# Reordering steps around each head's first scores, and the casts of the last head's output tiles

## The reference

```python
def diff_attend(q, k, v, lam):          # 8 heads, two softmax maps of 64 features each
    def block(qi):                      # 128 queries at a time
        s = jnp.einsum('bqhmd,bkhmd->bhmqk', qi, k).astype(jnp.float32) * scale
        p = jax.nn.softmax(s, axis=-1)
        a = (p[:, :, 0] - lam * p[:, :, 1]).astype(v.dtype)
        return jnp.einsum('bhqk,bkhd->bqhd', a, v)
...
ks_, qs: rope_2d for the latent tokens; k_all, v_all = cache (128 keys) + 512 latent keys
of = of * lax.rsqrt(jnp.mean(jnp.square(of), axis=-1, keepdims=True) + EPS) * subln_w
of = of * (1.0 - lam_init)
return of.astype(o.dtype).reshape(B, L, DA_V) @ w_o
```

## Time and profile before

| | us |
|---|---|
| median of the runs | 1765.52 |
| lowest, highest | 1765.09, 1766.39 |
| the profiled execution, its own time | 1772.52 |
| its span, first to last instruction | 1770.7 |
| TensorE busy in it | 1704.0 (96%) |
| VectorE, ScalarE, GpSimd busy | 1082.0, 703.2, 639.8 |
| attention heads, from the first scores to the last turned tile | about 59.8 to 357.3 |

### The profile page before, as it was taken

The page is one execution under the profiler, slowest core; times in us unless marked ns, Lnnn a source line. Parts: engine busy times, 40 slices in busy tenths (PEclk is TensorE's granted clock), DMA queues, the critical chain, the costliest instruction groups (busy, mean ns, idle before and its releaser), DMA issues.

```text
span 1770.7 us, 30194 instructions
## 1 busy us (share of the span) xinstructions
PE 1704.0 (96%) x11440; PEld 1601.7 (90%) x11440; DVE 1082.0 (61%) x1760; ACT 703.2 (40%) x1142; POOL 639.8 (36%) x317
## 2 busy tenths in 40 slices
PE   6999999899999999999999899999999999999996
PEld 4888888599998999889998899998999999999996
DVE  2677677757766515667367554645878771477824
ACT  4455555536323212232246544554463331133324
POOL 4222112256433433323454222123745333333344
PEclk8999999999999999999999999999999999999998
DMA  9312222521454223443221112211202222122221
GB/s 363 124 54 71 68 63 67 206 83 49 154 203 167 82 73 119 169 188 128 82 69 54 63 54 71 74 48 42 96 25 71 81 80 77 64 79 71 84 82 60
DMA packets 59768, 170.96 MB, mean 97 GB/s; under 512 B 7944, under 2 KB 20488, under 8 KB 59664
## 3 DMA queue, kind: packets, MB, share of 16 engines
q1 hardware_dynamic: 51584, 163.33, 26.6%
q10 hardware_dynamic: 8080, 6.18, 1.1%
HBM read 161.07 MB, written 4.74 MB: 94 GB/s over the span
## 4 chain that ended last, share of the span: by engine, by line
PE 69%; DVE 10%; ACT 6%; DVEq 5%; issue 4%; POOL 4%; ACTq 1%; DMA 1%; SPq 0%; POOLq 0%
PE pj L752 57%; POOL wlo L629 3%; DVEq L2298 2%; PE psO L1004 2%; PE mO L1237 2%; PE pfrow L777 1%; DVE pr L2312 1%; ACT pr L1569 1%; POOL ss L643 1%; PE psS L969 1%; DVE sm L2297 1%; DVEq L2311 1%; PE mS L1193 1%; ACT whi L1375 1%; PE psT L1012 1%
## 5 line engine op out<-in xcount | busy, mean ns | idle before, releaser
L591 POOL TENSOR_TENSOR wlo<-wraw,whi 128x1024 fp32r<-128x1024 f32 (+1 forms) x120 | 310.5, 2588 | 789.5 <-ACT whi L1375 787.4
L752 PE MATMUL pj<-Hh,whi 128*128 128x320 f32 x2240 | 536.7, 319 | 13.8 <-ACT Hh L1550 4.0
L752 PE MATMUL pj<-Hl,whi 128*128 128x320 f32 x2240 | 517.0, 311 | 1.4 <-POOL Hl L614 1.1
L752 PE MATMUL pj<-Hh,wlo 128*128 128x320 f32 x2240 | 518.1, 310 | 0.0
L752 PEld LDWEIGHTS pj<-Hh,whi 128*128 128x128 f32 x2240 | 375.6, 190 | 40.3 <-issue 29.7
L752 PEld LDWEIGHTS pj<-Hl,whi 128*128 128x128 f32 x2240 | 377.6, 189 | 2.4 <-POOL Hl L614 2.0
L752 PEld LDWEIGHTS pj<-Hh,wlo 128*128 128x128 f32 x2240 | 379.2, 189 | 0.3
L1375 ACT CAST whi<-wraw 128x1024 fp32r<-128x1024 f32 (+1 forms) x168 | 187.2, 1114 | 261.5 <-PE pj L752 227.7
L2218 DVE SCALAR_TENSOR_TENSOR fcv<-fus,vec,fcv 128x127 f32<-128x127 f32 (+1 forms) x176 | 222.3, 1304 | 15.1 <-issue 15.1
L752 PE MATMUL pj<-Gh,whi 128*128 128x320 f32 x704 | 168.5, 310 | 0.8 <-POOL wlo L629 0.8
L2080 DVE SCALAR_TENSOR_TENSOR X<-pj,mods,X 128x128 f32<-128x128 f32 (+5 forms) x114 | 43.1, 433 | 205.8 <-PE pj L752 205.6
(11 more groups left out here) (367 smaller groups left out, 2370.5 us busy)
## 6 DMA issues: line engine op xcount, KB each, us to landing
wraw<-in_w_up SPq DMA_DIRECT2D x84, 512.0 KB, 3.5
fwr<-in_w_ada SPq DMA_DIRECT2D x56, 512.0 KB, 5.2
wraw<-in_w_dn SPq DMA_DIRECT2D x32, 704.0 KB, 4.1
wraw<-in_w_qkv SPq DMA_DIRECT2D x24, 512.0 KB, 3.5
wraw<-in_w_mlin SPq DMA_DIRECT2D x24, 512.0 KB, 3.5
awr<-in_w_ada SPq DMA_DIRECT2D x16, 512.0 KB, 10.4
awr<-in_w_ada SPq DMA_DIRECT2D x16, 256.0 KB, 8.0
wraw<-in_w_wo SPq DMA_DIRECT2D x8, 512.0 KB, 3.6
```

Of the source, the lines that this page charges most:

```text
L591: nc.gpsimd.tensor_tensor(wlo[k][:, 0:width], wraw[k][:, 0:width], whi[k][:, 0:width].bitcast(F32), ALU.subtract).then_inc(w_lo, 1)
L752: last = mm(out[:, c, 0:HALF], w, x[:, j, c * HALF:(c + 1) * HALF], start=(j == 0 and n == 0), stop=(j == n_k - 1 and n == 2))
```

## The change

Five edits, all in layer 0's attention:

1. TensorE, `head` and `last_head`: step 7 of the query unit (in the last head: of the last value unit) goes ahead of `scores(h, 0)`.
2. VectorE, `head`: `turned(h, 3)` goes ahead of `q_lo(h + 1)`.
3. ScalarE, `last_head`: `unit_split(U_WO + 1)` goes from behind `o_square` to right behind `exps(h, 0)`.
4. ScalarE, `last_head`: the six `output_hi` casts move forward: tiles 0 and 1 behind `values_hi`, tile 2 behind `o_out(h - 1)`, tile 3 behind `exps(h, 2)`, tiles 4 and 5 behind `exps(h, 3)`.
5. GpSimd: the eight `Hl` subtractions are written out instead of a loop, and those of tiles 3, 4 and 5 wait for `nmax_ready` of score tiles 2, 3 and 4 of the last head as well.

```diff
+            def part_lo_split(n):
+                pool.wait_ge(part_hi, n + 1)
+                nc.gpsimd.tensor_tensor(wlo[0][:, 0:CUT * P], ...).then_inc(part_lo, 1)
...
-            output_lo(O32, 1, 0, KT)
+            for j in range(KT):
+                pool.wait_ge(h_hi, KT + j + 1)
+                if j in (3, 4, 5):
+                    pool.wait_ge(nmax_ready, 5 * (DA_HEADS - 1) + j)
+                nc.gpsimd.tensor_tensor(Hl[:, j, :], O32[:, j, :], Hh[:, j, :].bitcast(F32), ALU.subtract).then_inc(o_ready, 1)
+            part_lo_split(0)
...
+                qkv(q, [7])
                 scores(h, 0)
                 if h == 0:
                     ada_turn(3)
-                qkv(q, [7])
...
             def last_head(h):
+                qkv(3 * DA_HEADS - 1, [7])
                 scores(h, 0)
-                qkv(3 * DA_HEADS - 1, [7])
...
                 exps(h, 0)
+                unit_split(U_WO + 1)
                 values_hi(h)
+                output_hi(O32, onorm, (0, 1))
                 o_out(h - 1, (L0, L0 + LAT), 1)
+                output_hi(O32, onorm, (2,))
                 turned(h, 0)
                 exps(h, 1)
                 o_square(h - 1)
-                unit_split(U_WO + 1)
                 turned(h, 1)
                 exps(h, 2)
                 o_out(h, (C0, C0 + CTX), 0)
-                output_hi(O32, onorm, (0, 1))
+                output_hi(O32, onorm, (3,))
                 turned(h, 2)
                 exps(h, 3)
-                output_hi(O32, onorm, (2, 3))
+                output_hi(O32, onorm, (4, 5))
                 turned(h, 3)
                 exps(h, 4)
                 rms(h - 1)
-                output_hi(O32, onorm, (4, 5))
...
                 nmax(h, 4)
+                turned(h, 3)
                 q_lo(h + 1)
-                turned(h, 3)
                 k_lo(h + 1)
                 values_lo(h)
```

More of the change, by code:

```diff
@@ L607, in split_ffn @@
                 out_split(b + 2 * GH, n, WMAX, 0)
+            def part_lo_split(n):
+                pool.wait_ge(part_hi, n + 1)
+                nc.gpsimd.tensor_tensor(wlo[0][:, 0:CUT * P], wraw[0][:, 0:CUT * P], whi[0][:, 0:CUT * P].bitcast(F32),
+                                        ALU.subtract).then_inc(part_lo, 1)
             def output_lo(src, h_inst, n, early):
@@ L615, in output_lo @@
                 loop(pool, early, body)
-                pool.wait_ge(part_hi, n + 1)
-                nc.gpsimd.tensor_tensor(wlo[0][:, 0:CUT * P], wraw[0][:, 0:CUT * P], whi[0][:, 0:CUT * P].bitcast(F32),
-                                        ALU.subtract).then_inc(part_lo, 1)
+                part_lo_split(n)
                 for j in range(early, KT):
```

## The result

The changed kernel runs in 1761.82 us (median of 11 executions, 1758.1 to 1764.13). The kernel before, on the same chips in the same rounds, has 1771.19 (11 executions, 1765.09 to 1773.84). The ratio is 0.9949, 95% interval 0.9938 to 0.9961: 9.0 us faster, between 6.9 and 11.0. The forecast was 6.0 us faster. So the time lies inside the range that was given (1757.0 to 1762.8), the direction was right, and the gain was half as large again as forecast.

The account below looks back on a forecast made before the run. TensorE was taken as the bound (busy 1704.0 of 1770.7 us), gains coming from its idle time or clock. Heads 5.6 plus last head 0.5 gave 6.1; 6.0 off the 1765.5 median forecast 1759.5 us, range 1757.0 to 1762.8.

Parts of the forecast that it names:

- turned(3) ahead of q_lo: End of each head, VectorE: Al starts 0.46 us earlier, values_lo gains 0.3 to 0.38, rms moves to about 167.0.
- the chain: Between heads: Al, value transposes, GpSimd's split, combine(4), turn(4), its cast and its Al all move about 0.45 us earlier.
- Step 7 ahead of scores 0: Top of each head: query copy about 0.56 us earlier; both edits together 0.71 us per boundary, between 0.4 and 0.95.
- Rival A: Head boundaries: later maximum of score tile 0 holds Al back, each boundary worth 0.4 us; 1761.5 us in all; chance 0.2.
- The sum over the heads: All heads: 0.45 into head 1, 3.55 for heads 2 to 6, 0.38 into last, 1.2 in head 0; 5.6 us.
- The last head: Whole last head, step 7 and moved casts and subtractions: 0.5 us gained, between 1.5 lost and 2.2 gained.
- rival E: Last head: the wait for nmax on tiles 3 and 4 is already met when their casts are done; costs nothing.
- the lock at exps(1): Last head: early GpSimd subtractions delay score tile 1's scaling by 0.7 to 0.9 us; without it 0.6 us more gain.
- rival B: Last head: clock stays up, the 355 to 358 stretch at 0.53 goes, 1.4 us more gain, 1758.1 us; chance 0.12.
- both stretches: Last head: granted clock at 0.50 in 345 to 346 and 0.53 in 355 to 358, assumed to stay unchanged.
- C: Last head: new lock at 331 delays exps(1), next blocks at 0.50, later loads; 2 us lost, 1761.4 us; chance 0.12.
- D: Behind the last head: clock fall lasts into the dense output projection; 4.4 us slower, 1770 us; chance 0.04.

Follow-up runs that it names:

- tile 2 put off: Changed kernel with GpSimd's subtractions of tiles 3 and 4 put off past the next maximum and tile 2's past tile 1's scaling; 1759.82 us, ratio 0.9948.
- either edit alone: Changed kernel with subtractions of tiles 2, 3 and 4 put off: 1759.82 us; changed kernel with scores 4 ahead of piece 6 of last_blocks: 1761.25 us.
- both took the stage from 26.89 to 24.28 us: Changed kernel with subtractions of tiles 2, 3 and 4 put off and scores 4 ahead of piece 6 of last_blocks; 1760.64 us, ratio 0.9948.

## Why the prediction was right, and where it was short

**turned(3) ahead of q_lo.** Right in mechanism and size. Forecast 0.44 of the chain, measured 0.40 alone. Rms gets the new wait for values_lo that was named, 0.17 us.

**Step 7 ahead of scores 0.** Right in mechanism, too small in size: with the first edit it was to bring 0.71 us a head, and 0.85 were measured. Two terms make the 0.14. The part from the value transposes to the weights of values_lat was to shrink from 9.25 (174.00 - 164.75) to 8.99 (173.29 - 164.30), and is 8.90 (170.75 - 161.85), mostly because the weights follow 0.06 us behind the end of Al and not 0.12. The part ahead of the value transposes shrank by 0.50 and not by 0.45. Both ends of this term had been given (0.4 and 0.95), and the measured one lies between. Rival A wanted 37.1 or more between heads; 36.67 refutes it. The maximum of score tile 0 does come later (168.46), and does not hold Al back: the normalisation behind it ends at 169.92 and the cast that Al wants at 169.83. The wait of values_lat for Al, forecast at about 0.2 us, is 0.19.

**The sum over the heads.** From the value transposes of head 0 to those of head 6 it was 0.45 + 5 x 0.71 = 4.0, and is 6.33 - 1.59 = 4.74. For the top of head 0 it was 1.2, and 1.1 came: the shift is 1.34 us at its first turned tile, as the idle times in the earlier trace rows go, and 1.14 at the second, so the loss that was taken off did come: the small scaling of score tile 1 (67.25) meets GpSimd's split, which did not move, and lasts 0.36 us in place of 0.17. The 1.59 at its value transposes holds another 0.45 of turned(3), which the forecast counts in the boundary into head 1. (0.03 of each shift is older than attention.) At rms behind head 6, where the forecast stood at 5.6, the shift is 317.43 - 311.17 = 6.26. The 0.7 that is missing is five times the 0.14 from above.

**The last head.** 0.5 us was forecast for the whole of it, step 7 included, and from 6.26 to 7.74 at rms it is 1.5. This is the other term that was too small, by 1.0. The steps went as described, with other sizes. Step 7 brings 0.64 up to the value transposes (forecast 0.6). The scaling of tile 1 waits 0.42 us (forecast 0.7 to 0.9), that of tile 2 is free (0.72 as forecast); the three early subtractions end at 325.45, which is 332.35 with the 6.90 of shift (forecast 332.1); tiles 3 and 4 still meet combine (2.12 and 2.02 us), so rival E holds, at no cost, as the forecast took it. The load of `lwh` comes 0.3 us earlier.

But the load does not hide what VectorE gains, as the forecast had it: in after nothing waits for scores 4, and the maximum of tile 4 starts 23.95 us after the value transposes, against 24.42 with step 7 alone, where nothing waits for scores 4 either. That is 0.47 us for edits 3 to 5. These are the maxima of tile 4 with step 7 alone and, second, in the kernel before:

```profile
344.58 1.48 DVE L2297 TENSOR_REDUCE sm<-psS 128x2 f32<-128x1280 f32 x1
```

```profile
349.44 1.49 DVE L2297 TENSOR_REDUCE sm<-psS 128x2 f32<-128x1280 f32 x1 [0.28 <-PE psS L969]
```

In before it started at 24.77, 0.28 us of that idle for scores 4, which had run behind the late load and at half clock (344.2 to 347.6); that part is the clock's of one execution, in whole or in part. At equal clock after has 1.2 us more than the 6.9 of shift at the last head's value transposes, and the kernel with both edits to the heads has 6.6. So edits 3 to 5 seem worth 1 to 1.5 us on top of the other two, and 0.3 alone, with an error of 0.4 to 0.6 on each.

The Trainium skill, "SBUF — State Buffer", "SBUF: two separate sides", describes this lock between GpSimd and VectorE; the trace agrees both ways. Combine, with its two inputs in SBUF, lasts 2.12 us beside GpSimd and 0.89 alone. VectorE's maximum, whose one input is in PSUM, lasts 1.49 us at 323.32 in the middle of GpSimd's work, and 1.48 at 328.95 with GpSimd idle. The prediction also said that, without the lock at exps(1), most of the gain would still go to the late loads. With tile 2 put off that lock is gone and nothing comes earlier at rms, but half clock lies in that trace, so this is not shown.

**Clock.** Here the forecast was wrong for the profiled execution, and rival B, at a chance of 0.12, describes it: no stretch at half clock in the last head, and 1.53 us less behind rms (6.81 to 5.28), where B had 1.4. But B's reason, that the change keeps TensorE busier, isn't borne out. The second stretch of the earlier trace rows is missing too in the kernels with step 7 alone, turned(3) alone, and both, in which the clock falls once, near 340. And the kernel with the last head's edits alone has it at half clock from 338 to 345, without being slower than before. What changes from one execution to the next can't be a term of the sum. The step that failed is the sentence that left both stretches as they are: it treated one execution's clock as a property of the kernel. Over the executions the mean clock is the same for both (0.9896 and 0.9899), so the clock explains little of the 9.0 us of the ratio. The two profiled executions lie 0.006 of mean clock apart (0.987 and 0.993), and by the straight line that is about 7 of their 14.4 us.

**C and D.** Not in after. C's second half is seen, though, in the kernel with tile 2 put off: the clock was at 0.50 from 327.8, the next loads were asked for 1.2 us later, the weights came 2.75 us late, and the next blocks ran at 0.50 again. D did not occur in any trace: every stretch at half clock in the last head ended before the first product of `values_lat`.

**The sum again.** 6.26 over the heads and 1.48 in the last are 7.7 us, as the traces have it at rms, up to 0.35 of it clock; 8.1 at equal clock; 9.0 (6.9 to 11.0) by the ratio. These agree within their errors. The forecast of 6.0 lies just below the interval: its mechanism held, and it was too small by 0.7 us in the boundaries and 1.0 in the last head. Whether the last 1.3 us between 7.7 and 9.0 is anything but scatter stays open.

## What to carry to other kernels

Where the same short wait comes back in every round of a loop, work out its price once, for one distance between rounds, and check it there: 37.52 to 36.67 told more than the whole span did. Moving a wait away in a stage that has a second resource close behind (here a ring of loads) may pay only when the work behind that resource is moved too: either edit alone gave nothing here, and both took the stage from 26.89 to 24.28 us in one execution of each, 1.0 us of the time with an error of 0.6. Before a difference between two profiled executions is explained, follow one instruction through both: what arises where nothing was edited is not the change.

## What the runs showed of the hardware

The granted clock falls to 0.50 in stretches whose place and number differ between executions of the same code: behind attention, where nothing was edited, in five places of before and one of after. In after TensorE stood idle for 1.83 us from 325.4, and the clock stayed at 1.00; in the kernel with tile 2 put off as well it fell to 0.50 behind a stretch with 0.16 us of work in 2.00 (336.4 to 338.4). Taken over all executions, 0.001 of mean clock goes with 1.19 us of this kernel.

In these traces a lock shows as a longer instruction and not as idle time: the same combine lasts 0.89 us alone and 2.12 beside a subtraction of GpSimd that starts first and lasts 1.55, as it does alone (343.94).
